# One weight transfer of the last expert cut into three unequal partition groups

## What is computed

```python
def expert_choice_ffn(h, w_router, w_gate, w_up, w_down):
    cap = CAPACITY_FACTOR * s // N_EXPERTS          # 2 * 256 // 16 = 32 tokens for each expert
    aff = jax.nn.softmax((h @ w_router).astype(jnp.float32), axis=-1)
    gates, idx = lax.top_k(jnp.swapaxes(aff, 1, 2), cap)
    xs = jax.vmap(lambda hb, ib: hb[ib])(h, idx)
    hid = jax.nn.silu(jnp.einsum('becd,edf->becf', xs, w_gate)) * jnp.einsum('becd,edf->becf', xs, w_up)
    out = jnp.einsum('becf,efd->becd', hid, w_down) * gates[..., None].astype(h.dtype)
    return jax.vmap(lambda ob, ib: jnp.zeros((s, d), h.dtype).at[ib.reshape(-1)].add(ob.reshape(-1, d)))(out, idx)
```

## Time and profile before

| what | value |
|---|---|
| median of 3 runs | 2342.61 us (2340.86 to 2343.54) |
| the profiled execution's own time | 2339.89 us |
| its span | 2338.1 us |
| mean granted TensorE clock over the span | 0.883 of full speed |
| TensorE matmuls busy | 1836.8 us, 79% |
| VectorE, ScalarE, GpSimd busy | 34%, 23%, 4% |
| bytes over the DMA engines | 739.79 MB, of it 731.27 MB on SyncE's queue |

### The profile page before, as it was taken

The page is one execution under the profiler, slowest core; times in us unless marked ns, Lnnn a source line. Parts: engine busy times, 40 slices in busy tenths (PEclk is TensorE's granted clock), DMA queues, the critical chain, the costliest instruction groups (busy, mean ns, idle before and its releaser), DMA issues.

```text
span 2338.1 us, 28695 instructions
## 1 busy us (share of the span) xinstructions
PE 1836.8 (79%) x12606; PEld 1189.4 (51%) x12606; DVE 804.8 (34%) x1219; ACT 530.7 (23%) x800; POOL 89.6 (4%) x140
## 2 busy tenths in 40 slices
PE   7999999999999999998666666666666665666666
PEld 7888899998888998874221211222111211212221
DVE  4755667756566677662011001010100110010011
ACT  5644533356444335440000000000000000000000
POOL 1200000012100000010000000000000000000000
PEclk9999999999999999999788788787877777887787
DMA  7345657744445666359999999999999999999997
GB/s 245 127 153 172 192 198 249 235 147 138 164 149 189 222 229 207 127 233 385 430 428 429 430 430 427 429 430 429 428 428 430 429 429 429 430 430 428 429 429 315
DMA packets 171788, 739.79 MB, mean 316 GB/s; under 512 B 6752, under 2 KB 133216, under 8 KB 147088
## 3 DMA queue, kind: packets, MB, share of 16 engines
q1 hardware_dynamic: 169312, 731.27, 78.7%
q0 software_dynamic: 2352, 6.69, 0.9%
HBM read 736.88 MB, written 1.05 MB: 316 GB/s over the span
## 4 chain that ended last, share of the span: by engine, by line
DMA 48%; PE 41%; DVE 6%; ACT 3%; issue 2%; POOL 1%; SPq 0%; DVEq 0%; POOLq 0%; ACTq 0%
PE PS L335 40%; DMA WB<-in_w_down 24%; DMA WB<-in_w_up 23%; DVE WL L1575 2%; ACT WH L1054 1%; DVE X L1570 1%; POOL T L2321 1%; DMA S<-in_post_mix_g 1%; DVE S L1570 0%; PE PS L408 0%; DVE S L1567 0%; ACT HTh L1099 0%; DVE C L1570 0%; DMA W<-in_w_in 0%; DVE S L1642 0%
## 5 line engine op out<-in xcount | busy, mean ns | idle before, releaser
L335 PE MATMUL PS<-WB,XS 128*32 128x352 f32 x3072 | 364.0, 635 | 207.5 <-DMA WB<-in_w_up 120.7
L335 PE MATMUL PS<-WB,S 128*32 128x512 f32 x1408 | 267.2, 750 | 140.8 <-issue 72.9
L1575 DVE TENSOR_TENSOR WL<-W,WH 128x2048 fp32r<-128x2048 f32 x141 | 323.8, 2297 | 142.7 <-ACT WH L1054 142.6
L335 PEld LDWEIGHTS PS<-WB,XS 128*32 128x32 f32 x3072 | 116.8, 141 | 453.9 <-issue 171.9
L1570 DVE SCALAR_TENSOR_TENSOR S<-S,PS 128x352 f32<-128x352 f32 (+1 forms) x110 | 63.4, 588 | 790.2 <-ACT S L1540 753.9
L335 PE MATMUL PS<-HTh,WH 128*128 128x256 f32 x1064 | 309.9, 291 | 14.1 <-DVE HTl L1570 7.3
L1054 ACT ACTIVATE WH<-W 128x2048 fp32r<-128x2048 f32 x141 | 269.2, 1909 | 191.9 <-PE PS L335 191.0
L335 PE MATMUL PS<-HTl,WH 128*128 128x256 f32 x1064 | 305.4, 287 | 0.0
L335 PE MATMUL PS<-HTh,WL 128*128 128x256 f32 x1064 | 305.1, 287 | 0.0
L335 PEld LDWEIGHTS PS<-WB,S 128*32 128x32 f32 x1408 | 72.0, 126 | 326.7 <-issue 217.4
L335 PEld LDWEIGHTS PS<-HTh,WH 128*128 128x128 f32 x1064 | 208.4, 196 | 16.9 <-issue 9.9
(11 more groups left out here) (270 smaller groups left out, 2131.3 us busy)
## 6 DMA issues: line engine op xcount, KB each, us to landing
WB<-in_w_down SPq DMA_DIRECT2D x63, 2816.0 KB, 36.0
WB<-in_w_gate SPq DMA_DIRECT2D x48, 2816.0 KB, 35.9
WB<-in_w_up SPq DMA_DIRECT2D x48, 2816.0 KB, 35.5
C<-in_w_gate SPq DMA_DIRECT2D x16, 2816.0 KB, 36.1
C<-in_w_up SPq DMA_DIRECT2D x16, 2816.0 KB, 37.6
W<-in_w_in SPq DMA_DIRECT2D x31, 1024.0 KB, 5.4
S<-in_w_ada SPq DMA_DIRECT2D x24, 1024.0 KB, 5.4
W<-in_w_gate SPq DMA_DIRECT2D x22, 1024.0 KB, 7.9
```

Of the source, the lines that this page charges most:

```text
L335: return e.matmul(o, l, r, start=start, stop=stop, skip_group_check=True)
L1575: e.tensor_tensor(M.WL[i][:, :], M.W[:, 2048 * (m % NW):2048 * (m % NW) + 2048], M.WH[i][:, :].bitcast(F32), ALU.subtract).then_inc(*up("l ...
```

## The change

The third chunk (i = 2) of the last expert's down matrix is no longer one transfer of 128 partitions. It is issued as three transfers one after another, of partitions 0 to 48, 49 to 112 and 113 to 127. All three raise the same semaphore, each by 16, and the name that TensorE waits for stands for the value after the third. The bytes, the buffer, the wait ahead of the issue and the four pieces of the chunk behind it are as they were. No instruction of another engine changes.

```diff
@@ -188,6 +188,10 @@
 
 
 PIECES = ((0, 1, 2), (3, 4, 5), (6, 7, 8), (9, 10))
+
+
+
+UNEVEN = ((0, 49), (49, 113), (113, 128))
 
 
 class Memory:
@@ -2494,6 +2498,11 @@
                         lo, hi = 512 * piece[0], 512 * piece[-1] + 512
                         e.dma_start(buf[:, lo:hi], w[:, BIG * i + lo:BIG * i + hi]).then_inc(*up(f"piece{j}", 0, by=16))
                     continue
+                if (ex, wname, i) == (15, "w_down_2", 2):
+                    for j, (lo, hi) in enumerate(UNEVEN):
+                        to = up(sem, key, by=16) if hi == 128 else up(sem, key, j, by=16)
+                        e.dma_start(buf[lo:hi, :], w[lo:hi, BIG * i:BIG * i + BIG]).then_inc(*to)
+                    continue
                 e.dma_start(buf, w[:, BIG * i:BIG * i + BIG]).then_inc(*up(sem, key, by=16))
     for t in range(2):
         for h in range(2):
```

## The result

The changed kernel takes 2363.49 us (median of 4 runs, 2361.68 to 2368.07), the kernel before in the same comparison 2342.06 us (4 runs, 2340.86 to 2343.54). The ratio is 1.0096, with a 95% interval of 1.0084 to 1.0108: 21.4 us slower. The forecast was 2343.4 us and the range ended at 2348.0, so the prediction was wrong, and none of its rivals had this size either.

What follows compares the result with a forecast made beforehand. The weight stream was taken to bound the second half, late engines setting each landing. Issues 0, TensorE within slack and one row time, +0.84 us, on the runs' median 2342.61 gave 2343.4 us; range 2339.0 to 2348.0 us.

Steps and rivals of the forecast that it cites:

- What bounds the kernel: Second half: bound by the weight stream, 6.72 us for a chunk, 0.84 us for a row; late engines set every landing.
- Issues at no cost: SyncE's queue: two more issues of 0.33 us fit in its 7.6 us wait for a buffer, so 0.
- Rows for each engine: Cut chunk and pieces: busiest engine gets 9 rows for 8, +0.84 us; equal shares give -2.5 or +3.4 us.
- The least uneven division: Cut chunk's rows shared as whole rows, 4 + 4 + 1 = 9 on the busiest engine: +0.84 us if late, else 0.
- the +0.84: Last piece's landing: one row time later, taken as the forecast's sum, in us.
- What the pace belongs to: Late engines' writes: pace is the engine's or the written partitions'; if the partitions', 0 to +2.5 us, +0.84 us taken.
- The sentence on the Trainium skill's table: Write ports: late ports keep their rows and the 15 rows meet on four ports, 0 to +2.5 us.
- Rival B: Chunk 2 and piece landings: seven loaded engines among the late eight, +3.4 us, up to +5.9 if rows meet; chance 0.27.
- Rival A: End of stream: equal shares, pace the engines' own, seven loaded engines early; -2.5 us, 2340.1 us; chance 0.27.
- Rival C: Cut chunk: odd sizes not shared out, 68 rows on one engine, +50.4 us if late, 2384 to 2393; chance 0.04.
- TensorE's part: Matmuls from chunk 2 on: 1.5 to 2 us of slack, which just holds some 1.5 us of slower clock after idling.
- the prediction's guess: Late half of the engines: likely delayed by 100 instruction packets (1.64 MB, 16 KB each) that share the engines.

Runs made afterwards that it cites:

- the even cut: Chunk cut into 48, 64 and 16 neighbouring partitions, eight rows for each engine, against the kernel before: 2361.57 us, ratio 1.0087.
- On expert 1: The 49, 64, 15 cut on the third chunk of expert 1's down matrix, none on the last expert's, against the kernel before: 2358.16 us, ratio 1.0075.

## Why the prediction was wrong, point by point

- *What bounds the kernel* held. The stream sets the pace, and one transfer that lands late moves the end by as much: the cut chunk landed 22.9 us later and the span grew by 22.6. The row of 0.84 us is in the packets themselves, and the two halves are in the steps of the last piece's semaphore: eight at 2316.2 to 2318.6 us, eight at 2324.1 to 2326.0. So the halves are some 8 us apart, and 9.8 us from the first engine to the last.
- *Issues at no cost* held: three transfers along the floats cost nothing.
- *Rows for each engine.* The equal shares are what the chip does. SyncE's queue has 169334 packets where the kernel before has 169312, with the same rows. With one small packet for each engine that takes part, these 22 are 7 + 16 + 15 in place of 16, and the cut chunk's semaphore has 38 = 7 + 16 + 15 steps behind 2300 us in the trace. The least uneven division, one of the two supports of the +0.84, isn't used (16 + 16 + 15 would have given 31 packets more). The rule of the Trainium skill that the prediction named for this agrees, number by number (partition cuts of two, three, four and eight transfers with even shares have 16, 32, 48 and 112 packets more than the kernel before). The counts don't say which engines take part. This is the smaller fault: by the prediction's own terms it was worth 3.4 us at most, and even shares cost as much as uneven ones. In the division itself the prediction slipped too: with seven engines at 12 rows and one at 4 it is eight engines that have 5, not "seven or eight", since 128 - 84 - 4 = 40.
- **The step that failed is "What the pace belongs to".** It named the branch that came true, that the pace belongs to the partitions written, but it priced that from one place only, the late engines' own rows: the work there stays, so 0, with three row times (+2.5 us) as the upper end and one (+0.84 us) as the value taken. It left out that the cut sends *all* engines to write where others are at work, those of the cut rows and those still on the chunk ahead. Rows that meet took some 1.7 us each and more, and there were 205 of them and not one to three. The term measured 21.4 us in place of 0.84. The sentence on the Trainium skill's table had the same fault: it looked at the 15 rows and gave 0 to +2.5 us. Applied to all three transfers, that table gives the 49 rows only 8 of the 16 ports and the 64 rows (49 to 112) only 12, too few for 16 engines to have one each.
- *Rival B* had its condition (late engines among the seven, if the 49 rows take the first seven) and not its size, +3.4 to +5.9 us. *Rival A* lacked both of its conditions: the pace was not the engines' own, and two of the first seven engines are late. *Rival C*, one engine alone, would have shown a share of 0.06; the share was near 1.
- *The range* was built from counts of rows at 0.84 us each. Once a row may take 2 us on the mean, and rows of the uncut chunk ahead are slowed too, counts don't bound the cost. An unseen way of writing should have kept the upper end open.
- *TensorE's part*: the prediction's slower clock behind an idle time was there (0.50 from 2322 us on, after the idle time that began near 2316), and cost nothing that can be seen: from the cut chunk's landing to the end it was 18.7 us against 19.0 before.

**What stays open.** The rule says which cuts cost, and the packets say that each costly cut with even shares makes some 200 rows slow, over 32 to 35 us. Not worked out is why it is about 200 whether 16 or 64 rows are split off, and so why the cost is two and a half to three times the 6.7 us of the chunk. A half whose 64 rows meet two by two would by itself take twice 3.4 us, so two halves would cost 6.7 us more; 18.5 were measured. The chunk ahead of the cut is slowed as well. That engines which have come to the cut rows hold up those still on the chunk ahead fits this, but no view shows which engine writes where. That the unequal shares cost something of their own isn't excluded: the change and the even cut are both at +21.4 us, each with an interval of some 3 us on either side. No version here is faster than the kernel before. Whether a cut that keeps the groups even can also move rows to early engines was not tried. What makes eight engines late was not tried either, but the trace of the kernel before speaks for the prediction's guess. From the chunk that lands first at 1182 us to the one at 2309 us 39 instruction packets of 16 KB were moved, about 1.0 to 1.1 us each and mostly with one row of some 1.34 us beside it. The engines' lags behind the first one, added up, grew from 14 to 77 us, 1.6 us for each packet.

## What to carry to other kernels

When a weight stream saturates the DMA engines, cut a transfer along the free dimension, or in steps of 2 or 4 over all partitions, and not into blocks of neighbouring partitions: one such cut in 192 chunks cost 17 to 21 us here, and in the change it slowed the unchanged transfer ahead of it too. Read the DMA share beside the rate: half the rate at half the share is idle engines, half the rate at full share was, here, engines in each other's way. And where a change makes a transfer of a shape that the trace doesn't have, bound its cost by what it can do to its neighbours, not only by its own rows.

## What the runs showed of the hardware

- With 15.5 engines at work the stream moved 171 GB/s, 11.0 GB/s for each, against 26.8 GB/s for each in order; a row took 2.04 us on the mean and not 0.84.
- Where the rows are read from did not matter: read in halves and written in stripes cost nothing (1.0002).
- On expert 1, slow rows (over 1.4 us) ran from 1175.7 to 1202.6 us, 192 of them, and then each row took 0.84 us again; the engines stayed further apart to the end (16.3 us at the last piece, 9.8 in the kernel before).
- The engines drift apart over the stream though all have the same rows: the steps of one chunk's semaphore lie 2.0 us apart near 1095 us and 9.8 near 2302. The late ones are not one half in a row but the sixth, the seventh and the tenth to fifteenth, in the order in which small loads take them.
